# The end of a streamed mixture of experts: the last pair's gate and up stage goes ahead of the last but one pair's down stage

## What is computed

```python
top_v, top_e = lax.top_k(logits, 4)              # 4 of 32 experts per token
gates = softmax(top_v)
gate, up = split(x_rows @ w_gu[e] + b_gu[e])     # w_gu: 32 x 1024 x 2048 f32
gate, up = minimum(gate, 7), clip(up, -7, 7)
y_rows = ((up + 1) * gate * sigmoid(1.702 * gate)) @ w_d[e] + b_d[e]   # w_d: 32 x 1024 x 1024
x = x + gt2 * sum_over_the_4(gates * y_rows)
y = rmsnorm(x, g_final)
```

## Time and profile before

| | us |
|---|---|
| median of three executions | 1258.83 |
| lowest, highest | 1255.25, 1260.27 |
| the profiled execution, its own time | 1258.83 |
| its span | 1257.2 |
| TensorE busy in it | 1167.6 (93%) |
| granted TensorE clock, mean | 0.982 |
| DMA of the weights' queue, share of 16 engines | 92.2% |

### The profile page before, as it was taken

One profiled execution on the slowest core, in us unless ns is written; L12 is line 12 of the kernel. 1 busy time (PEld: TensorE's weight loads), 2 busy tenths in 40 slices (PEclk: granted clock), 3 DMA queues, 4 the chain that ended last, 5 costly groups with the idle time before them and its releaser, 6 DMA issues.

```text
span 1257.2 us, 15278 instructions
## 1 busy us (share of the span) xinstructions
PE 1167.6 (93%) x6018; PEld 587.3 (47%) x6018; DVE 329.7 (26%) x605; ACT 175.5 (14%) x345; POOL 48.4 (4%) x95
## 2 busy tenths in 40 slices
PE   7999999999999999889899989898988989899996
PEld 4788756778643443424243434333342424243333
DVE  3289975523221031011111110111021011102133
ACT  3133232100210200200020002001000200020102
POOL 1032121100000000000000000000000000000000
PEclk9999999999999999999989999999999999999999
DMA  9998999997799999999999999999999999999994
GB/s 339 360 367 312 373 337 383 388 411 266 296 382 431 426 428 427 429 428 430 427 428 429 426 427 427 430 426 428 430 428 429 428 429 429 428 427 429 422 416 174
DMA packets 70948, 500.66 MB, mean 398 GB/s; under 512 B 8969, under 2 KB 11091, under 8 KB 41964
## 3 DMA queue, kind: packets, MB, share of 16 engines
q1 hardware_dynamic: 64096, 478.38, 92.2%
q0 software_dynamic: 6576, 21.42, 4.8%
q10 hardware_dynamic: 220, 0.09, 0.0%
HBM read 496.48 MB, written 3.38 MB: 398 GB/s over the span
## 4 chain that ended last, share of the span: by engine, by line
PE 68%; DMA 26%; ACT 2%; DVE 2%; issue 1%; SPq 0%; DVEq 0%
DMA ring<-in_w_d 23%; PE ps L1039 21%; PE ps L1112 12%; PE ps L507 12%; PE ps L1215 4%; PE ps L988 3%; DMA ring<-in_w_gu 3%; PE ps L412 2%; PE ps L853 2%; PE ps L906 2%; PE ps L938 1%; PE ps L464 1%; PE ps L701 1%; PE ps L1004 1%; ACT oT L1510 1%
## 5 line engine op out<-in xcount | busy, mean ns | idle before, releaser
L1039 PE MATMUL ps<-ring,zone 128*64 128x512 f32 x1520 | 424.1, 596 | 6.5 <-DMA ring<-in_w_gu 5.3
L1112 PE MATMUL ps<-ring,oT 128*64 128x512 f32 x768 | 238.8, 623 | 37.1 <-DMA ring<-in_w_d 19.7
L1039 PEld LDWEIGHTS ps<-ring,zone 128*64 128x64 f32 x1520 | 134.8, 138 | 229.7 <-issue 225.9
L2107 DVE TENSOR_SCALAR zone<-ps 128x1024 f32<-128x1024 f32 x15 | 18.4, 1225 | 517.5 <-PE ps L1039 517.5
L507 PE MATMUL ps<-early,ring 128*128 128x264 f32 x640 | 150.7, 392 | 1.7 <-DVE early L1670 1.4
L1112 PEld LDWEIGHTS ps<-ring,oT 128*64 128x64 f32 x768 | 73.2, 143 | 156.9 <-issue 129.8
L507 PEld LDWEIGHTS ps<-early,ring 128*128 128x128 f32 x640 | 120.6, 192 | 30.6 <-issue 9.7
L1039 PE MATMUL ps<-zone 128*64 128x512 f32 x272 | 109.5, 593 | 5.6 <-DMA ring<-in_w_gu 5.6
L1039 PE MATMUL ps<-early,zone 128*64 128x512 f32 x240 | 98.9, 593 | 0.0
L1500 ACT ACTIVATE attn<-zone 128x1024 f32<-128x1024 f32 x15 | 15.8, 1057 | 451.5 <-DVE zone L2107 451.5
L1039 PEld LDWEIGHTS ps<-zone 128*64 128x64 f32 x272 | 33.6, 137 | 77.0 <-issue 68.2
(11 more groups left out here) (392 smaller groups left out, 946.2 us busy)
## 6 DMA issues: line engine op xcount, KB each, us to landing
ring<-in_w_gu SPq DMA_DIRECT2D x95, 2048.0 KB, 26.9
ring<-in_w_d SPq DMA_DIRECT2D x45, 2048.0 KB, 22.4
zone<-in_w_gu SPq DMA_DIRECT2D x16, 2048.0 KB, 27.0
early<-in_w_gu SPq DMA_DIRECT2D x15, 2048.0 KB, 29.6
ring<-in_w_ada SPq DMA_DIRECT2D x12, 2048.0 KB, 12.2
ring<-in_w_in SPq DMA_DIRECT2D x18, 1024.0 KB, 11.3
early<-in_w_d SPq DMA_DIRECT2D x8, 2048.0 KB, 23.9
zone<-in_w_d SPq DMA_DIRECT2D x7, 2048.0 KB, 22.5
```

What stands on the lines that cost most here:

```text
L1039: ins = pe.matmul(ps[64 * j:64 * j + CAP, c, :], xg[:, k, 2 * par + j, :], rows, start=False, stop=(k == KT - 1), skip_group_check=True)
L1112: ins = pe.matmul(ps[64 * j:64 * j + CAP, 4 + c, :], hidT[:, k, j * CAP:(j + 1) * CAP], w[j][:, kk, c * 512:(c + 1) * 512], start=(k == 0) ...
L2107: V.tensor_scalar(gate_v, ps[:, 0:2, :].rearrange("p a b -> p (a b)"), LIMIT, None, ALU.min).then_inc(sig("gate_ready"), 1)
```

## The change

The last pair's gate/up loads and products go ahead of pair 0's down loads and products, on SyncE and on TensorE. Pair 0's second two down matrices are loaded in pieces of 512 KB too (its first two stay whole), and pair 1's as before. The last pair's turned rows go to `last_hidT`, which lies in `attn`, where the sigmoids were. Since pair 0's down products now come right before pair 1's, `final_row` and both turns stand between pair 0's k steps 4 to 6, and `half_products` between pair 1's k steps 0 to 4. VectorE uses the whole-row `swiglu` for the last pair in place of the one in halves, and folds `into_tokens` between the additions.

```diff
--- before
+++ after
@@ names @@
+        last_hidT = attn_flat[:, 0:KT * P].rearrange("p (k c) -> p k c", c=P)
@@ TensorE: turn_last_hidden @@
-                if g == 0:
-                    pe.wait_ge(sig("hid_half"), rnd + 1)
-                else:
-                    pe.wait_ge(sig("hid_ready"), q * 2 + 2)
+                pe.wait_ge(sig("hid_ready"), q * 2 + 2)
                 pe.wait_ge(sig("g_taken"), rnd * 2 + (g + 1))
@@ TensorE: down loses its arguments edge, rnd and in_rows, and what they chose; new: @@
+            def last_down(rnd, q, par):
+
+                pe.wait_ge(sig("ye_ready"), q * 2 + par)
+                hidden = last_hidT if par else hidT
+                for k in range(KT):
+                    s, kk = k // 4, k % 4
+                    if kk == 0:
+                        pe.wait_ge(sig("read"), q * 10 + (5 + 4 * par + s))
+                        slots = [expert_load("dn", 2 * s + j, q, par, par == 1)[1] for j in range(2)]
+                        w = [places[slot][:, 0:4096].rearrange("p (k c) -> p k c", k=4) for slot in slots]
+                    if par == 0 and k in (4, 5):
+                        final_row(q, k - 4)
+                    if par == 0 and k == 6:
+                        turn_last_hidden(rnd, q, 0)
+                        turn_last_hidden(rnd, q, 1)
+                    if kk < 3 and (par, s) != (0, 0):
+                        pe.wait_ge(sig(f"late{6 * par + 3 * s - 3 + kk}"), rnd * 32 + 32)
+                    elif kk in (0, 3):
+                        for j in range(2):
+                            expert_slot("dn", 2 * s + j, q, par, par == 1)
+                    for c in range(2):
+                        for j in range(2):
+                            ins = pe.matmul(ps[64 * j:64 * j + CAP, 4 + c, :], hidden[:, k, j * CAP:(j + 1) * CAP],
+                                            w[j][:, kk, c * 512:(c + 1) * 512],
+                                            start=(k == 0), stop=(k == KT - 1), skip_group_check=True)
+                            if kk == 3 and c == 1:
+                                ins.then_inc(sig("slots_used"), 1)
+                        if par == 1 and k == KT - 1 and c == 0:
+                            ins.then_inc(sig("down_half"), 1)
+                    if par == 1 and k < 5:
+                        half_products(rnd, q, range(max(0, 2 * k - 1), min(KT, 2 * k + 1)))
@@ TensorE: final_row, half_products @@
-            def final_row(rnd, g):
-                pe.wait_ge(sig("half_added"), rnd * 2 * KT + (KT + 7 + g))
+            def final_row(q, g):
+                pe.wait_ge(sig("read"), q * 10 + (7 + g))
...
                         pe.wait_ge(sig("ye_ready"), q * 2 + 1)
-                        pe.wait_ge(sig("read"), q * 10 + (7 + m))
-                        if m == 0:
-                            pe.wait_ge(sig("read"), q * 10 + 8)
+                        pe.wait_ge(sig("read"), q * 10 + (9 + m))
@@ TensorE: last_quad @@
                 def between(s):
                     if s == 0:
                         turn_put(q, True)
-                    elif s == 1:
-                        half_products(rnd, q, range(6))
-                    elif s == 2:
-                        half_products(rnd, q, range(6, KT))
 
                 gate_up(q, 0, False, False)
                 early_half(rnd, q)
-                down(q - 1, 1, False, False)
+                down(q - 1, 1)
                 turn_hidden(q, 0, False, rnd)
                 combine(q - 1, (1,))
-                down(q, 0, True, False)
-                gate_up(q, 1, True, False, between=between, by_tile=True)
-                final_row(rnd, 0)
-                final_row(rnd, 1)
-                turn_last_hidden(rnd, q, 0)
-                down(q, 1, True, False, rnd, in_rows=True)
+                gate_up(q, 1, False, False, between=between, by_tile=True)
+                last_down(rnd, q, 0)
+                last_down(rnd, q, 1)
                 pe.wait_ge(sig("ye_half"), rnd + 1)
                 for m in range(KT):
                     if m == 4:
                         pe.wait_ge(sig("ye_ready"), q * 2 + 2)
+                    if m >= 6:
+                        pe.wait_ge(sig("half_added"), rnd * 2 * KT + (KT + m + 1))
                     final_products(m).then_inc(sig("summed"), 1)
@@ ScalarE: take_last_hidden writes last_hidT; last_quad @@
                 sigmoid(q, 0)
                 take_output(q - 1, 1)
                 take_hidden(q, 0)
-                take_output(q, 0, True)
                 take_put(q, True)
-                act.wait_ge(sig("gate_half"), rnd + 1)
-                nc.scalar.activation(sig_v[:, 0:512], gate_v[:, 0:512], ACT.Sigmoid, scale=ALPHA)\
-                    .then_inc(sig("sig_half"), 1)
+                sigmoid(q, 1)
                 for g in range(2):
...
-                take_last_hidden(q, 0)
-                act.wait_ge(sig("gate_ready"), q * 2 + 2)
-                nc.scalar.activation(sig_v[:, 512:1024], gate_v[:, 512:1024], ACT.Sigmoid, scale=ALPHA)\
-                    .then_inc(sig("sig_ready"), 1)
-                take_last_hidden(q, 1)
+                for g in range(2):
+                    take_last_hidden(q, g)
+                take_output(q, 0)
@@ VectorE: last_swiglu is gone; last_quad @@
                 set_put(q, qq)
                 add_quad(q - 1)
+                V.memset(eps_col, EPS)
+                swiglu(q, 1, False)
+
+                def into_tokens(m):
+                    dve.wait_ge(sig("half_added"), rnd * 2 * KT + (KT + m + 1))
+                    V.scalar_tensor_tensor(out=xT[:, m, 0:TP], in0=acc[:, m, 0:TP], scalar=modT[:, 40 + m, 0:1],
+                                           in1=xT[:, m, 0:TP], op0=ALU.mult, op1=ALU.add)
+
                 for m in range(KT):
                     dve.wait_ge(sig("half_summed"), rnd * 2 * KT + (KT + m + 1))
                     V.tensor_tensor(acc[:, m, :], acc[:, m, :], ps[:, 6 + m % 2, 0:T], ALU.add)\
                         .then_inc(sig("half_added"), 1)
-                V.memset(eps_col, EPS)
-                dve.wait_ge(sig("half_added"), rnd * 2 * KT + 2 * KT)
-                for m in range(KT):
-                    V.scalar_tensor_tensor(out=xT[:, m, 0:TP], in0=acc[:, m, 0:TP], scalar=modT[:, 40 + m, 0:1],
-                                           in1=xT[:, m, 0:TP], op0=ALU.mult, op1=ALU.add)
+                    if m:
+                        into_tokens(m - 1)
+                into_tokens(KT - 1)
...
-                last_swiglu(rnd, q)
@@ SyncE: load_last_down(q, par), load_round @@
+                            expert = 2 * (PAIRS - 2 + par) + j
+                            if (par, s_) == (0, 0):
+                                if kk == 0:
+                                    sp.dma_start(places[slot][:, 0:4 * D], dn[expert, s_, :, :])\
+                                        .then_inc(landed[slot], 16)
+                                continue
                             sp.dma_start(places[slot][:, kk * D:(kk + 1) * D],
-                                         dn[2 * (PAIRS - 1) + j, s_, :, kk * D:(kk + 1) * D])\
-                                .then_inc(landed[slot] if kk == 3 else sig(f"late{3 * s_ + kk}"), 16)
+                                         dn[expert, s_, :, kk * D:(kk + 1) * D])\
+                                .then_inc(landed[slot] if kk == 3 else sig(f"late{6 * par + 3 * s_ - 3 + kk}"), 16)
...
                 load_expert("gu", last, QUADS - 1, 0, False)
                 load_expert("dn", last - 1, QUADS - 2, 1, False)
-                load_expert("dn", last, QUADS - 1, 0, True)
-                load_expert("gu", last, QUADS - 1, 1, True, by_tile=True)
-                load_last_down(last)
+                load_expert("gu", last, QUADS - 1, 1, False, by_tile=True)
+                load_last_down(last, 0)
+                load_last_down(last, 1)
```

More of the change, by code:

```diff
@@ L1090, in turn_put, with down @@
                     ins.then_inc(sig("filled"), 1)
-            def down(q, par, edge, cold, rnd=0, in_rows=False):
+            def down(q, par, cold=False):
                 n = q * 2 + par
@@ L1099, in down @@
                     if kk == 0:
[L1100 to L1109, removed]
+                        pe.wait_ge(sig("read"), q * 10 + (5 + 2 * par + s))
+                        w = [expert_slot("dn", 2 * s + j, q, par, False)[:, 0:4096].rearrange("p (k c) -> p k c", k=4)
+                             for j in range(2)]
                     for c in range(2):
@@ L1116, in down @@
                                 ins.then_inc(sig("slots_used"), 1)
-                        if in_rows and k == KT - 1 and c == 0:
+            def last_down(rnd, q, par):
[25 more added lines that the diff above has]
+                        if par == 1 and k == KT - 1 and c == 0:
                             ins.then_inc(sig("down_half"), 1)
-            def final_row(rnd, g):
-                pe.wait_ge(sig("half_added"), rnd * 2 * KT + (KT + 7 + g))
```

(28 more changed lines are left out.)

## The result

| | us |
|---|---|
| before, median of 6 executions | 1256.49 (1254.91 to 1260.27) |
| after, median of 6 executions | 1264.51 (1263.33 to 1266.09) |
| ratio after to before | 1.0055, 95% interval 1.0033 to 1.0077 |
| the profiled execution after, its own time and its span | 1264.80, 1263.1 |

What follows compares the result with a forecast made beforehand. Loads and TensorE were taken as nearly equal, TensorE ending the products at 1242.2. Work and waits to 1246.7 plus 1.6 of clock gave 1248.3, 6.1 later; with the tail and 1.63 around the span, 1264.9, range 1259.8 to 1268.0.

Steps and rivals of the forecast that it cites:

- three signs of being wrong: Landing near 1209 coming by 1204, TensorE reaching it later than 1205, or TensorE waiting for the last pair's pieces.
- The stretch: From landing of the quad before's last down matrix to the first final_products; its end was forecast 6.1 us later.
- The wait for two whole matrices: After the last gate/up products, TensorE idle 6.1 us, 1203.4 to 1209.5, for pair 0's first two down matrices.
- The clock: Behind that idle time, pair 0's first 32 down records run at about half clock, costing 1.6 us.
- The handover: Between pair 0's and pair 1's down products, TensorE waits 1.25 us for ScalarE's copies out of banks 4 and 5.
- The products themselves: Down products of pair 0 and pair 1 at the end, priced at 13.93 us each.
- second sum: Cross-check from 1172.3: 66.8 us of work plus 1.1, 6.1, 1.25 and 1.6 of waits and clock, giving 1249.1.
- `half_products` and `final_row`: Helpers among the last down products: eight half_products at 4.65 us, two final_rows at 2.05, both turns at 1.36.
- The loads: Last pieces land at 1240.2 and hold nobody; six more issues, smaller pieces costing 0.4 us.
- What could be won: Loads alone allow products to end near 1241.6, against 1242.2 before: at most 0.6 us from reordering the last quad.
- The rival in which the loads set the end in both orders: Pair 0's first two down matrices there by 1203.4, no idle time or clock loss: 1258.6 us; chance 0.06.
- the rival with the longer stretch at half clock: Clock down twice as long in pair 0's down products, 1.6 us more, and landing 1.0 later: 1267.5; chance 0.20.

Runs made afterwards that it cites:

- e2: Changed kernel with pair 0's first two down matrices loaded in 512 KB pieces too; 1258.20 us, ratio 1.0007 to the kernel before.
- e5: Changed kernel with 50 identity transposes, results unread, put in TensorE's idle time ahead of pair 0's down products; 1260.79 us.
- e3: Changed kernel with all four of pair 0's down matrices as whole loads, only pair 1's in pieces; 1267.47 us.
- e4: Changed kernel with pair 0's down products in banks 0 and 1, so pair 1's in banks 4 and 5 needn't wait; 1262.06 us.
- e6: Changed kernel with all pair 0 down matrices in pieces, both final_rows before pair 0's first k, pair 0's down products in banks 0 and 1; 1257.98 us.
- e8: Kernel before, with the last pair's down products leaving out the right half of the columns for k 0, 1 and 2; 1255.01 us.
- e1: Changed kernel with 20 identity transposes, results unread, put in TensorE's idle time ahead of pair 0's down products; 1264.70 us.
- e7: Changed kernel, loads kept whole, with both final_rows and both turns put in the idle time ahead of pair 0's down products; 1260.18 us.

## Why the prediction was right

It gave 1264.9 and the runs gave 1264.51, within half a per cent of the 1258.83 that it started from. The mechanism is right: the idle time, the fall of the clock, the wait for ScalarE and the chain's last landing came as it said, and none of its three signs of being wrong did. That the time is within 0.4 us is luck: it started 2.3 us above the median of the six executions of before and forecast a loss 1.9 us too small. From 1256.49 it would have given 1262.6. The stretch was forecast 6.1 us longer (83.7 to 89.8) and came out 7.4 longer (83.7 to 91.1), while what lies ahead of it was 1.3 us shorter in the profiled execution after than in the one before (1157.17 against 1158.50), which the change doesn't touch. Against the medians the change costs 8.0 us where 6.1 were forecast. Point by point:

- **The wait for two whole matrices**: forecast as 6.1 us of idle time behind a landing 51.0 us into the stretch; 6.2 us and 50.7. Right, and e2 shows it to be the cause: without it the changed order takes 84.6.
- **The clock**: forecast as 1.6 us, from the wait of 2.6; 2.0 here (9.13 against 7.09 in e5). The step was right and undersized. Over the runs with the long wait (the changed kernel, e3 and e4) it was 2.0, 2.9 and 2.5 us. What the Trainium skill says there (TensorE: Matmul & The Clock Gate, "HAM oscillation — how this bites in real kernels"), that a wait for the next slice leaves the following burst cold, held in each of these. In the kernel before, at 914, it did not the earlier trace rows. The case that the section of the Trainium skill describes has waits of some 3 to 5 us; the prediction held it against waits of 2.6 to 2.8 us, which are shorter, so that its count of two rows for and one against tests the rule only loosely.
- **What the rows on the clock left out**: rows 8 and 9 show three waits of 2.6 to 2.8 us for a down matrix. The trace of the kernel before has thirteen of them, 2.58 to 2.81 us long. Behind eight the next 4 us had a clock of 0.57 to 0.64, and behind five, at 501, 511, 855, 914 and 924, it stayed at 1.00, with waits just as long. For a wait of 2.6 us the fall was thus a matter of eight in thirteen; none of these rows says what 6 us do. The three executions with 6.2 or 6.3 us all fell to 0.50.
- **The handover**: forecast 1.25 us, measured 1.2, and shown to be on the path by e4.
- **The products themselves**: this term was too small, and it is nearly the whole of what the forecast of the stretch missed. The 128 down records of both pairs took 31.2 us, 29.2 without the clock's 2.0, where the prediction had twice 13.93, so 27.9. A k step of the down products that is followed by another form takes 1.87 us, or 1.94 behind a wait, and 13.93 / 8 = 1.74 in a long row, and the changed order has some ten such joints. The prediction priced changes of form only for `half_products`. Its second sum, which starts from the measured work of the old stretch, was nearer: products to 1249.1 are a stretch of 90.6, and with the clock's 2.0 it is 91.0 of the measured 91.1. The 0.8 us that it left out as small gaps should have stayed in.
- **`half_products` and `final_row`**: 0.65 + 3 x 1.10 + 0.65 = 4.6 against 4.65, and 2.2 against 2.05. The turns took 1.17 in place of 1.36.
- **The loads**: the last landing was forecast at 1240.2, 81.7 us into the stretch, and in the changed kernel the stream is down to 8 GB/s from 1238 to 1240; e6, where the last landing can be read, has it at 82.0. Six more issues and the smaller pieces cost nothing that e3 could show.
- **What could be won**: 0.6 us by the prediction's bound. e8 wins 0.4 by the stretch, and e6, with all three defects of the changed order mended, ends where the kernel before does (84.1 against 83.7, and no difference of the times outside the interval). The 0.4 is small beside what one execution can tell; that 2.6 us less work brought no more is the stronger half of the reading.

The rival in which the loads set the end in both orders didn't happen in the changed kernel, but it is what e6 became: it needed TensorE to begin pair 0's down products by 1203.4, and pieces made that possible where no faster landing could. Of the rival with the longer stretch at half clock, e3 shows the most: 2.9 us of clock, short of the 3.2 that the rival had.

## What to carry to other kernels

Where the loads and the products are nearly equal in length, an order is judged by what the consumer needs at each landing: moving the heavy consumer (here gate/up, 28 us of products) ahead leaves it running dry in front of the next load, and this idle time comes back in full at the end. The first load behind such a point should be small, so that work starts with its first piece; 512 KB in place of 2 MB there was worth 6.5 us, of which 2.0 were the clock. Price a long idle time of TensorE with the clock that it loses, and each interleaved helper with its joint of 0.13 us; before reordering a tail at all, compare its end with its last landing, for the difference is all that can be won.

## What the runs showed of the hardware

- 32 down records cost 7.09 us at the full clock and 8.78, 9.13, 9.63 and 10.04 us behind idle times of 3.9, 6.2, 6.3 and 6.2 us (e1, the changed kernel, e4 and e3): the same wait of 6.2 or 6.3 us cost between 2.0 and 2.9 us of clock, in three kernels that are alike for TensorE up to it.
- The clock can fall in the idle time or behind it. In the changed kernel it was at 0.83 and 0.50 while TensorE was still idle; in e1 and e7 it was at 1.00 through the whole idle time (3.9 and 2.99 us) and at 0.60 and 0.73 in the window behind it.
- Waits of 2.58 to 2.81 us in the kernel before were followed by a window at 0.57 to 0.64 in eight of thirteen cases and at 1.00 in five; the length of the wait doesn't tell which.
- Idle time split by work didn't keep the clock in e7 (longest idle time 2.99 us). It stayed in e5 (50 transposes of the identity, 0.73 us left) and in e2 and its waits of up to 0.7 us.
- Twenty transposes of the same 128x128 identity took 2.40 us, 0.12 each; the eight of the turns took 1.17, 0.15 each.
- The first product behind the landing came 50.8 to 51.2 us into the stretch in the five executions that have pair 0's first matrices whole and nothing in their way (the changed kernel, e1, e3, e4 and e5), while the landing at the stretch's start lay anywhere between 1154.9 and 1158.7 us over all runs. Much of the spread of the whole times (5.4 us over the six executions of before) comes from ahead of the part that was changed.
